# Ten convolution taps as products on ScalarE, added by VectorE, and a re-ordered head of the program

## The chip, the core and the metric

The kernel runs on one core of a Trainium2 chip. A core has TensorE (matrix products into PSUM, eight banks of 128x512 f32), VectorE, ScalarE, GpSimd, and SyncE, which issues most DMAs. Each engine runs its own instructions in order; they meet through semaphores. The metric is the device time of one execution, in microseconds (us); lower is better.

## The reference

Two transformer blocks on 256 tokens of width 1024, f32. Only what the change touches is shown: the first block's input projections, rotation and depthwise convolution of 31 taps over 512 channels.

```python
def conformer_conv(u, kernel, bias, ln_g, ln_b):
    a, b = jnp.split(u, 2, axis=-1)
    h = a * jax.nn.sigmoid(b)
    pad = CONV_WIDTH // 2
    h = lax.conv_general_dilated(h, kernel[:, None, :].astype(h.dtype), window_strides=(1,),
                                 padding=[(pad, pad)], dimension_numbers=('NWC', 'WIO', 'NWC'),
                                 feature_group_count=CONV_DIM) + bias
    hf = h.astype(jnp.float32)
    mu = jnp.mean(hf, axis=-1, keepdims=True)
    var = jnp.mean(jnp.square(hf - mu), axis=-1, keepdims=True)
    hn = (hf - mu) * lax.rsqrt(var + EPS) * ln_g + ln_b
    return jax.nn.silu(hn).astype(u.dtype)
...
        mod_x = (silu_c @ w_ada[i] + b_ada[i])[:, None, :]
        hx = modulate(rms_norm(x, norm1_g[i]), sh1, sc1)
        hc = modulate(rms_norm(ctx, norm1_g[i]), csh1, csc1)
        qx, kx, vx, ux = split_proj(hx @ w_in[i])
        kvc = hc @ w_in[i][:, ATT_DIM:3 * ATT_DIM]
        qx_rot = axial_rope(qx, row_pos, col_pos)
        kx_rot = axial_rope(kx, row_pos, col_pos)
        attn_x = neighbourhood_attention(qx_rot, qx, kx_rot, vx, kc, vc, rpb[i])
        conv_x = conformer_conv(ux, dw_kernel[i], dw_bias[i], conv_ln_g[i], conv_ln_b[i])
        x_new = x + g1 * (jnp.concatenate([attn_x, conv_x], axis=-1) @ w_out[i])
```

## The kernel before

Every large product is made in three: weights and activations are split into a high part (fp32r) and the rest, and TensorE adds high x high, high x low and low x high into one bank (`part`, lines 414 to 416). ScalarE makes the high part of each weight block (`hi`, line 1005), VectorE the low part (`lo`, line 1480). Weight blocks travel through a ring of six slots and their high buffers, in an order fixed by the list `slots`. A block is fetched by SyncE when the one before it in its slot has been used. TensorE's order is written out by hand, and so are those of VectorE and ScalarE.

The head goes by eight feature blocks of 128. For each, TensorE makes the modulation from an ada block of 1 MB (`mod_first`, line 454), VectorE copies the rows out (`rows_out`, line 1520), TensorE turns them (`mod_turn`, lines 465 and 468), VectorE applies them (`modulate_x`), ScalarE makes the high part (`high_x`), VectorE the low part (`low_x`), and TensorE uses the block for the convolution's two input halves a and b (`ab`, lines 490 to 496). Until the first weights are there, TensorE multiplies a tile of ones (`keep_busy`, line 476). After the eight blocks the context's rows are normalised (squares on ScalarE, line 1017; power on GpSimd; scaling `hat` on VectorE, line 1492) and the key weights are split.

Then TensorE runs the projections in this order: k of x, k of the context (KC), q, v of the context (VC), the first half of V. ScalarE copies each finished bank out, in the same order. Then TensorE turns KC, Q, KR and QR (line 396), two turns each, in banks 6, 7, 2, 3, 6, 7, 2, 3. A bank is free again when ScalarE has copied the turned tile: kcT (KC), qT (Q), kT (KR), qrT (QR). So KR's turn waits for kcT's copy, QR's for qT's. The first scores (`scores1(0)`, line 577) need all eight copies and stand between the two halves of the last product with V.

Beside all this the convolution runs on VectorE. `hp` holds the padded input by channel: 4 blocks of 128 channels, 288 columns. ScalarE makes tap 0 with the bias for each block (line 1074). VectorE adds the other 30 taps, each a fused multiply and add of 128x256 into `cacc`, four blocks in turn, 120 instructions (`taps`, line 1495). 20 follow the rotation of the keys (KR), 8 more the low parts of four weight halves, 52 the rotation of the queries (QR), 4 the first softmax step, and 36 are spread over the first five of eight attention steps.

Of the kernel before, what the change touches and what calls it, by code (L numbers as in the profile page):

```python
# [24 lines left out]
class Mem:  # L25


    def __init__(self, nc, ctx):
# [165 lines left out]
def weight_units(d, S):  # L194
# [70 lines left out]
    slots = [2, 4, 3, 5, 12, 0, 13, 1, 2, 4, 3, 5, 12, 0, 13, 1, 2, 3, 4, 5, 0, 1]  # L265
# [44 lines left out]
def pool_program(e, m, S, d):  # L310
    w = Waits(e)

    def power(i):
# [52 lines left out]
def tensor_program(e, m, S, by):  # L366
# [58 lines left out]
    def mod_unit(unit, k0, bk, sem):  # L425
# [19 lines left out]
    def mod_first(e8):  # L445
# [544 lines left out]
def scalar_program(e, m, S, units, by, out, d):  # L990
# [472 lines left out]
def vector_program(e, m, S, units, by):  # L1463
# [809 lines left out]
```

## Time and profile before

| | us |
|---|---|
| three timed runs | 736.58, 737.40, 737.42 (median 737.4) |
| profiled execution | 736.31 |
| its span on the core | 734.5 |
| TensorE busy | 722.9 |
| VectorE busy | 508.9 |
| ScalarE busy | 398.0 |
| GpSimd busy | 25.0 |
| granted TensorE clock, mean | 0.998 |

The profiled execution's own time lies 1.8 us above its span. A share of busy time tells how full an engine is, not whether it holds up the others. TensorE is full; only where it waits can an edit change the time, or where a new wait arises.

### The profile page before, as it was taken

What the parts mean: (1) busy time and instruction counts of PE and PEld (TensorE: products, weight loads), DVE (VectorE), ACT (ScalarE), POOL (GpSimd) and SP (SyncE); (2) the same over time, 40 slices, a digit from 0 to 9 for tenths busy, and PEclk for the clock granted to TensorE, in tenths of its full rate; (3) what the DMA queues carried; (4) which work ended last, traced back from release to release, by engine and by line L of the source; (5) the groups of instructions that cost most, each with busy time, mean ns of one, the idle gap of its engine ahead of it and who ended that gap; (6) DMA issues with size and microseconds to landing.
All of it is one profiled execution on the core that took longest, in us unless ns stands there. A gap on an engine that the chain in (4) does not pass through costs nothing.

```text
span 734.5 us, 9784 instructions
## 1 busy us (share of the span) xinstructions
PE 722.9 (98%) x3824; PEld 578.6 (79%) x3824; DVE 508.9 (69%) x924; ACT 398.0 (54%) x662; POOL 25.0 (3%) x44
## 2 busy tenths in 40 slices
PE   8989999999999999999999999999999999999996
PEld 7668885568888888888878777778888888888885
DVE  4678999889667555565988799865857445544544
ACT  3366337886666545556545677666466344334432
POOL 1030012000100000000010000000000000000000
PEclk9999999999999999999999999999999999999999
DMA  9993939945464655445538533344366555655511
GB/s 365 415 354 117 374 112 360 368 161 176 159 223 158 229 192 209 172 163 182 159 101 302 200 115 115 117 176 167 114 230 205 195 175 188 209 175 172 172 58 57
DMA packets 73741, 144.90 MB, mean 197 GB/s; under 512 B 4112, under 2 KB 27664, under 8 KB 72672
## 3 DMA queue, kind: packets, MB, share of 16 engines
q1 hardware_dynamic: 71888, 138.98, 54.6%
q0 software_dynamic: 1520, 5.03, 1.9%
q8 instruction: 30, 0.49, 0.3%
q10 hardware_dynamic: 288, 0.27, 0.1%
q14 instruction: 15, 0.12, 0.1%
HBM read 143.22 MB, written 1.05 MB: 196 GB/s over the span
## 4 chain that ended last, share of the span: by engine, by line
PE 93%; DVE 3%; issue 2%; ACT 1%; POOL 1%; POOLq 0%; DVEq 0%
PE bank L414 22%; PE bank L416 22%; PE bank L415 22%; PE bank L735 5%; PE bank L396 5%; PE bank L733 3%; PE bank L433 2%; PE bank L476 1%; PE bank L454 1%; PE bank L577 1%; PE bank L490 1%; DVE WL L1480 1%; PE bank L599 1%; PE bank L852 1%; PE bank L874 1%
## 5 line engine op out<-in xcount | busy, mean ns | idle before, releaser
L1480 DVE TENSOR_TENSOR WL<-W,WH 128x1024 fp32r<-128x1024 f32 (+2 forms) x222 | 249.5, 1169 | 48.8 <-ACT WH L1005 48.5
L1005 ACT ACTIVATE WH<-W 128x1024 fp32r<-128x1024 f32 (+2 forms) x222 | 211.7, 1011 | 52.9 <-DMA W<-in_w_mlp 40.5
L414 PE MATMUL bank<-WH,AHL 128*128 128x512 f32 (+1 forms) x480 | 189.2, 394 | 2.3 <-DVE WL L1480 2.0
L416 PE MATMUL bank<-WH,AHL 128*128 128x512 f32 (+1 forms) x480 | 185.4, 386 | 0.0
L415 PE MATMUL bank<-WL,AHL 128*128 128x512 f32 (+1 forms) x480 | 185.2, 386 | 0.0
L414 PEld LDWEIGHTS bank<-WH,AHL 128*128 128x128 f32 x480 | 90.2, 188 | 24.0 <-DVE WL L1480 3.5
L416 PEld LDWEIGHTS bank<-WH,AHL 128*128 128x128 f32 x480 | 90.1, 188 | 18.7
L415 PEld LDWEIGHTS bank<-WL,AHL 128*128 128x128 f32 x480 | 90.3, 188 | 16.8
L414 PE MATMUL bank<-WH,HH 128*128 128x512 f32 (+1 forms) x218 | 84.9, 390 | 0.0
L416 PE MATMUL bank<-WH,HL 128*128 128x512 f32 (+1 forms) x218 | 84.5, 388 | 0.0
L415 PE MATMUL bank<-WL,HH 128*128 128x512 f32 (+1 forms) x218 | 84.4, 387 | 0.0
L735 PE MATMUL bank<-AHL,WH 128*128 128x512 f32 x168 | 60.5, 398 | 0.0
L733 PE MATMUL bank<-AHL,WL 128*128 128x256 f32 x192 | 50.0, 281 | 0.0
L1495 DVE SCALAR_TENSOR_TENSOR cacc<-hp,vec,cacc 128x256 f32<-128x256 f32 x120 | 48.3, 475 | 0.0
L416 PEld LDWEIGHTS bank<-WH,HL 128*128 128x128 f32 x218 | 40.9, 188 | 8.5
L415 PEld LDWEIGHTS bank<-WL,HH 128*128 128x128 f32 x218 | 41.0, 188 | 8.3
L414 PEld LDWEIGHTS bank<-WH,HH 128*128 128x128 f32 x218 | 40.9, 188 | 8.0
L1412 ACT ACTIVATE rel<-bank 128x256 f32<-128x256 f32 x22 | 8.5, 384 | 62.2 <-PE bank L416 61.0
L1489 DVE TENSOR_TENSOR hid<-bank,rel 128x256 f32<-128x256 f32 x22 | 9.3, 424 | 42.2 <-ACT rel L1412 42.2
L733 PEld LDWEIGHTS bank<-AHL,WL 128*128 128x128 f32 x192 | 36.3, 189 | 2.0
L735 PEld LDWEIGHTS bank<-AHL,WH 128*128 128x128 f32 x168 | 31.6, 188 | 6.7
L1780 DVE TENSOR_TENSOR HL<-bank,HH 128x256 fp32r<-128x256 f32 (+1 forms) x26 | 11.1, 461 | 30.9 <-ACT HH L1013 30.9
(265 smaller groups left out, 831.4 us busy)
## 6 DMA issues: line engine op xcount, KB each, us to landing
W<-in_w_mlp SPq DMA_DIRECT2D x32, 1024.0 KB, 5.5
W<-in_w_in SPq DMA_DIRECT2D x24, 1024.0 KB, 5.1
W<-in_w_ada SPq DMA_DIRECT2D x12, 1024.0 KB, 8.0
WX<-in_w_ada SPq DMA_DIRECT2D x12, 1024.0 KB, 9.9
W<-in_w_gate SPq DMA_DIRECT2D x22, 512.0 KB, 4.2
W<-in_w_up SPq DMA_DIRECT2D x22, 512.0 KB, 5.3
W<-in_w_down SPq DMA_DIRECT2D x11, 1024.0 KB, 5.0
W<-in_w_out SPq DMA_DIRECT2D x8, 1024.0 KB, 5.1
```

Of the source, the lines that this page charges most:

```text
L396: ins = e.transpose(bank[b][:, c * 128:c * 128 + 128], src, m.ident[:, :])
L414: e.matmul(po, hs, wh[:, k, c0:c0 + cw], start=first and k == 0, stop=False)
L415: e.matmul(po, hs, wl[:, k, c0:c0 + cw], start=False, stop=False)
L416: ins = e.matmul(po, ls, wh[:, k, c0:c0 + cw], start=False, stop=last and k == unit.nk - 1)
L433: ins = e.matmul(bank[bk][32 * g:32 * g + 32, :], m.csp[:, k0 + g, :], wv[:, g, :], start=k0 == 0, stop=k0 == 4, tile_position=(0, 32 * g))
L733: ins = e.matmul(bank[4 + j][:, 0:256], wl[:, k, js], m.AH[:, 4 * i + k, :], start=False, stop=False)
L735: ins = e.matmul(both, wh[:, k, js], m.AHL[:, :, 4 * i + k, :], start=False, stop=i == 1 and k == 3)
L1005: e.activation(m.WH[unit.slot][:, c], m.W32[unit.slot][:, c], ACT.Copy).then_inc(S["w_hi"], 1)
L1480: e.tensor_tensor(m.WL[unit.slot][:, c], m.W32[unit.slot][:, c], m.WH[unit.slot][:, c].bitcast(F32), ALU.subtract).then_inc(S["w_lo"], 1)
L1489: e.tensor_tensor(o, a, b, op).then_inc(S[sem], 1)
L1495: e.scalar_tensor_tensor(o, a, scalar, b, op0, op1).then_inc(S[sem], 1)
L1780: e.tensor_tensor(L[:, k0:k0 + nj, ts], bank[b][:, 0:nj * 128].rearrange("p (j n) -> p j n", j=nj), H[:, k0:k0 + nj, ts].bitcast(F32), ALU ...
```

## The change

The convolution: taps 21 to 30 no longer run as 40 fused instructions. ScalarE makes each as four products of 128x256 (`tap_products`) into one of two buffers, `cprod`, and VectorE adds all four channel blocks with one addition of 128x1024 (`add_product`). Product n waits until addition n-2 has read the buffer. The buffers lie on memory that `U` and `V` use, so the copy of V waits for all ten additions. The products stand between ScalarE's bank copies. VectorE has 60 taps and the ten additions ahead of the first softmax, and 20 taps behind.

The head: the context is fetched two blocks earlier. ScalarE squares it ahead of feature block 6 and splits the key weights right behind block 7; VectorE scales its two halves ahead of block 7's row copy and between the low parts of the two key blocks. Five of the first 16 products of ones go, and the four behind the first ada block. Two slots change places in the list. Some semaphores are merged under new names, their counts moved accordingly (`gate_u` and `g_sig` to `gate_sig`, `kr` and `qr` to `rotated`, `eps` and `csp` to `setup`, `ones` and `hp_zero` to `fills`, `last_sum` and `x_g` to `last_rows`); those lines are left out here.

```diff
+        self.cprod = [M(f"cprod{i}", (68, 56)[i], [128, 4, 256]) for i in range(2)]
...
+CONV_PRODUCTS = 10
...
-    slots = [2, 4, 3, 5, 12, 0, 13, 1, 2, 4, 3, 5, 12, 0, 13, 1, 2, 3, 4, 5, 0, 1]
+    slots = [2, 4, 12, 5, 3, 0, 13, 1, 2, 4, 12, 5, 3, 0, 13, 1, 2, 3, 4, 5, 0, 1]
...
-    for n in range(16):
+    for n in range(14):
         load(n)
     e.dma_start(m.XC[:, :, :], d["ctx"].rearrange("(t p) n -> p t n", p=128)).then_inc(S["l_xc"], 16)
-    for n in range(16, len(units)):
+    for n in range(14, len(units)):
         load(n)
...
-    keep_busy(16)
+    keep_busy(11)
     mod_first(0)
-    keep_busy(4)
     mod_turn(0)
     keep_busy(8)
...
-    for k in range(8):
+    for k in range(6):
         hi()
         high_x(k)
     w.wait_ge(S["l_xc"], 16)
     for tb in range(2):
         square(2 + tb, m.XC[:, tb, :], m.XC2[:, tb, :])
     hi()
-    w.wait_ge(S["eps"], 1)
+    high_x(6)
     e.activation(m.stat[:, 92:93], m.stat[:, 94:95], ACT.Sigmoid)
+    hi()
+    high_x(7)
+    hi(2)
     for tb in range(2):
         w.wait_ge(S["b_mm"], 15 + tb)
-        e.activation(m.G[:, tb, :], bank[2 + tb][:, :], ACT.Sigmoid).then_inc(S["gate_u"], 1)
-    hi()
+        e.activation(m.G[:, tb, :], bank[2 + tb][:, :], ACT.Sigmoid).then_inc(S["gate_sig"], 1)
...
+    def tap_products(*ns):
+
+        for n in ns:
+            j = 31 - CONV_PRODUCTS + n
+            if n > 1:
+                w.wait_ge(S["conv_add"], n - 1)
+            else:
+                w.wait_ge(S["u_turned" if n == 0 else "c_turned"], (2, 4)[n])
+            for c in range(4):
+                e.activation(m.cprod[n % 2][:, c, :], m.hp[:, c, j:j + 256], ACT.Copy,
+                             scale=m.dw[:, c, j:j + 1]).then_inc(S["conv_prod"], 1)
+
+    tap_products(0, 1)
     for tb in range(2):
         from_bank("k_mm", 6 + 2 * tb, m.KC[:, tb, :], tb, slice(0, 512), "kc_out")
+        if tb == 0:
+            tap_products(2)
     hi(2)
+    tap_products(3)
     for tb in range(2):
         from_bank("q_mm", 2 + 2 * tb, m.Q[:, tb, :], 2 + tb, slice(0, 512), "q_out", 0.125)
+        tap_products(4 + 2 * tb, 5 + 2 * tb)
...
     for tb in range(2):
         from_bank("v_mm", 2 * tb + 2, m.VC[:, tb, :], 4 + tb, slice(0, 512), "vc_out")
+        tap_products(8 + tb)
     qk_features(0, m.kcT)
     qk_features(1, m.qT)
+    w.wait_ge(S["conv_add"], CONV_PRODUCTS)
     from_bank("v_mm", 6, m.V[:, 0, :], 0, slice(0, 512), "v_out")
     qk_features(2, m.kT)
     qk_features(3, m.qrT)
...
         low_x(k)
+        if k == 6:
+            mean_square(2, (2,))
+            hat(m.XC, m.XC2, 0, 2, "c_hat")
+    lo()
+    mean_square(3, (3,))
+    hat(m.XC, m.XC2, 1, 3, "c_hat")
+    lo()
     for tb in range(2):
-        mean_square(2 + tb, (2 + tb,))
-        hat(m.XC, m.XC2, tb, 2 + tb, "c_hat")
-    lo(2)
-    for tb in range(2):
-        w.wait_ge(S["gate_u"], tb + 1)
+        w.wait_ge(S["gate_sig"], tb + 1)
...
+    def add_product():
+
+        w.wait_ge(S["conv_prod"], 4 * conv["added"] + 4)
+        w.wait_ge(S["conv_first"], 4)
+        w.wait_ge(S["conv"], conv["n"] - 4)
+        w.wait_ge(S["conv_add"], conv["added"])
+        cv = flat(m.cacc[:, :, :])
+        tt(cv, cv, flat(m.cprod[conv["added"] % 2][:, :, :]), ALU.add, "conv_add")
+        conv["added"] += 1
...
-    rope1(m.KR, m.Kt, "kr")
-    taps(20)
+    rope1(m.KR, m.Kt, "rotated")
+    taps(8)
+    add_product()
+    add_product()
+    taps(8)
     lo(2)
+    add_product()
+    taps(4)
+    add_product()
+    w.wait_ge(S["q_out"], 2)
+    w.wait_ge(S["rotated"], 1)
+    rope1(m.QR, m.Q, "rotated")
+    for _ in range(4):
+        taps(6)
+        add_product()
     taps(8)
-    w.wait_ge(S["q_out"], 2)
-    w.wait_ge(S["kr"], 1)
-    rope1(m.QR, m.Q, "qr")
-    taps(52)
+    add_product()
+    add_product()
+    taps(8)
...
-        taps((9, 8, 8, 7, 4, 0, 0, 0)[u])
+        taps((6, 5, 4, 3, 0, 0, 0, 0)[u])
```

On ScalarE, from the first tap to the copy of the turned queries, this stood before (WH<-W are high parts of value weights):

```order
L1074 ACTIVATE cacc<-hp,vec 128x256 x4
L1013 ACTIVATE KC<-bank 128x512 x2
L1005 ACTIVATE WH_61<-W_0_49 128x1024 x2
L1005 ACTIVATE WH_62<-W_1_50 128x1024 x2
L1013 ACTIVATE Q<-bank 128x512 x2
L1013 ACTIVATE VC<-bank 128x512 x2
L1013 ACTIVATE kcT<-bank 128x512 x2
L1013 ACTIVATE qT<-bank 128x512 x2
L1013 ACTIVATE V<-bank 128x512
L1013 ACTIVATE kT<-bank 128x512 x2
L1013 ACTIVATE qrT<-bank 128x512 x2
```

In the changed kernel, from the second query copy on (products 4 and 5 stand ahead of it; `cprod_119` and `cprod_120` are the two product buffers):

```order
L1014 ACTIVATE Q<-bank 128x512
L1088 ACTIVATE cprod_119<-hp,vec 128x256 x4
L1088 ACTIVATE cprod_120<-hp,vec 128x256 x4
L1014 ACTIVATE VC<-bank 128x512
L1088 ACTIVATE cprod_119<-hp,vec 128x256 x4
L1014 ACTIVATE VC<-bank 128x512
L1088 ACTIVATE cprod_120<-hp,vec 128x256 x4
L1014 ACTIVATE kcT<-bank 128x512 x2
L1014 ACTIVATE qT<-bank 128x512 x2
L1014 ACTIVATE V<-bank 128x512
L1014 ACTIVATE kT<-bank 128x512 x2
L1014 ACTIVATE qrT<-bank 128x512 x2
```

Product 5 has moved in ahead of the second copy of Q, products 8 and 9 around the second copy of VC and so ahead of kcT.

On VectorE, from the end of the keys' rotation to the first softmax, before:

```order
L1489 TENSOR_TENSOR KR<-KR,tmp 128x1024
L1495 SCALAR_TENSOR_TENSOR cacc<-hp,vec,cacc 128x256 x20
L1480 TENSOR_TENSOR WL_55<-W_0_49,WH_61 128x1024 x2
L1480 TENSOR_TENSOR WL_56<-W_1_50,WH_62 128x1024 x2
L1495 SCALAR_TENSOR_TENSOR cacc<-hp,vec,cacc 128x256 x8
L1489 TENSOR_TENSOR QR<-Q,rope_78 128x1024
L1489 TENSOR_TENSOR tmp<-Q,rope_78 128x16x16 x4
L1489 TENSOR_TENSOR QR<-QR,tmp 128x1024
L1495 SCALAR_TENSOR_TENSOR cacc<-hp,vec,cacc 128x256 x52
```

In the changed kernel, from the end of the queries' rotation to the first softmax:

```order
L1517 SCALAR_TENSOR_TENSOR cacc<-hp,vec,cacc 128x256 x6
L1511 TENSOR_TENSOR cacc<-cacc,cprod_119 128x1024
L1517 SCALAR_TENSOR_TENSOR cacc<-hp,vec,cacc 128x256 x6
L1511 TENSOR_TENSOR cacc<-cacc,cprod_120 128x1024
L1517 SCALAR_TENSOR_TENSOR cacc<-hp,vec,cacc 128x256 x6
L1511 TENSOR_TENSOR cacc<-cacc,cprod_119 128x1024
L1517 SCALAR_TENSOR_TENSOR cacc<-hp,vec,cacc 128x256 x6
L1511 TENSOR_TENSOR cacc<-cacc,cprod_120 128x1024
L1517 SCALAR_TENSOR_TENSOR cacc<-hp,vec,cacc 128x256 x8
L1511 TENSOR_TENSOR cacc<-cacc,cprod_119 128x1024
L1511 TENSOR_TENSOR cacc<-cacc,cprod_120 128x1024
L1517 SCALAR_TENSOR_TENSOR cacc<-hp,vec,cacc 128x256 x8
```

Behind the rotation of Q there are now 40 taps and six additions where 52 taps were.

On VectorE at the end of the head, from the low part of feature block 7 on, before (XC is the context, `S_95` the features):

```order
L1489 TENSOR_TENSOR AHL<-S_95,AHL 128x256
L1506 TENSOR_SCALAR stat<-stat 128x1
L1492 TENSOR_SCALAR XC_109<-XC,stat 128x1024
L1506 TENSOR_SCALAR stat<-stat 128x1
L1492 TENSOR_SCALAR XC_109<-XC,stat 128x1024
L1480 TENSOR_TENSOR WL_57<-W_2_51,WH_63 128x1024 x2
```

In the changed kernel, with the first context scaling ahead of block 7's row copy:

```order
L1511 TENSOR_TENSOR AHL<-S_95,AHL 128x256
L1528 TENSOR_SCALAR stat<-stat 128x1
L1514 TENSOR_SCALAR XC_109<-XC,stat 128x1024
L1542 COPY rows_7_107<-bank 128x256
...
L1511 TENSOR_TENSOR AHL<-S_95,AHL 128x256
L1502 TENSOR_TENSOR WL_57<-W_2_51,WH_63 128x1024 x2
L1528 TENSOR_SCALAR stat<-stat 128x1
L1514 TENSOR_SCALAR XC_109<-XC,stat 128x1024
L1502 TENSOR_TENSOR WL_58<-W_3_52,WH_64 128x1024 x2
```

The scaling of the context has moved to either side: one ahead of `rows_7`, one between the low parts of the two key weight blocks.

## Rows read from the trace of the kernel before

**Rows 1.** The page, part 1: busy us (share of the span) xinstructions.
```profile
PE 722.9 (98%) x3824; PEld 578.6 (79%) x3824; DVE 508.9 (69%) x924; ACT 398.0 (54%) x662; POOL 25.0 (3%) x44
```

**Rows 2.** TensorE's waits: waiting line, releaser: us in total, times, longest.
```profile
PE bank L414 <- DVE WL L1480: 2.0, 1, 2.0
PE bank L490 <- ACT AHL L1013: 0.3, 1, 0.3
```

**Rows 3.** Busy us by engine (instructions), then clock, DMA share, GB/s; one stage.
```profile
57.45:101.99 44.54, 44.54 (x204) 36.91 (x203) 41.86 (x83) 18.11 (x28) 0.00 (x0) 1.00 0.60 216
```

**Rows 4.** Timeline of TensorE at the start: start us, us, engine, line, count.
```profile
2.76 6.40 PE L476 MATMUL bank<-ones 128*128 128x128 f32 x32 [2.76 <-POOL ones L334]
11.53 1.95 PE L476 MATMUL bank<-ones 128*128 128x128 f32 x16
```

**Rows 5.** Issue of the last ada block, and its us to landing.
```profile
27.14 0.43 SPq L294 DMA_DIRECT2D WX<-in_w_ada  x1
...
WX<-in_w_ada SPq DMA_DIRECT2D x1, 1024.0 KB, 9.4
```

**Rows 6.** Timeline, 41 to 50 us, of VectorE, ScalarE, TensorE; idle before in brackets.
```profile
41.23 0.42 DVE L1520 COPY rows<-bank 128x256 f32<-128x256 f32 x1
...
42.62 0.38 PE L468 MATMUL bank<-ident,rows 128*128 128x128 f32 x2
...
44.55 1.04 ACT L1017 ACTIVATE XC<-XC 128x1024 f32<-128x1024 f32 x1
...
46.53 0.75 DVE L1492 TENSOR_SCALAR XC<-XC,stat 128x1024 f32<-128x1024 f32 x1 [0.67 <-POOL stat L317]
...
48.68 2.35 DVE L1480 TENSOR_TENSOR WL<-W,WH 128x1024 fp32r<-128x1024 f32 x2
...
49.95 0.50 PE L414 MATMUL bank<-WH,AHL 128*128 128x512 f32 x1 [2.04 <-DVE WL L1480]
```

**Rows 7.** Timeline of VectorE in the convolution stage.
```profile
66.42 1.23 DVE L1489 TENSOR_TENSOR KR<-Kt,rope 128x1024 f32<-128x1024 f32 x1 [0.19 <-ACT Kt L1013]
...
69.02 1.22 DVE L1489 TENSOR_TENSOR KR<-KR,tmp 128x1024 f32<-128x1024 f32 x1
...
78.10 4.62 DVE L1480 TENSOR_TENSOR WL<-W,WH 128x1024 fp32r<-128x1024 f32 x4
...
86.49 1.22 DVE L1489 TENSOR_TENSOR QR<-Q,rope 128x1024 f32<-128x1024 f32 x1 [0.60 <-ACT Q L1013]
...
90.23 20.69 DVE L1495 SCALAR_TENSOR_TENSOR cacc<-hp,vec,cacc 128x256 f32<-128x256 f32 x52
```

**Rows 8.** Timeline of ScalarE in the same stage.
```profile
66.16 2.08 ACT L1074 ACTIVATE cacc<-hp,vec 128x256 f32<-128x256 f32 x4
...
85.86 0.60 ACT L1013 ACTIVATE Q<-bank 128x512 f32<-128x512 f32 x1 [4.84 <-PE bank L416]
...
102.62 1.09 ACT L1013 ACTIVATE kcT<-bank 128x512 f32<-128x512 f32 x2 [5.28 <-PE bank L396]
```

**Rows 9.** ScalarE's groups by form: names, shapes, count | busy us, mean ns.
```profile
L1005 ACT ACTIVATE WH<-W 128x1024 fp32r<-128x1024 f32 x202 | 200.8, 1052 | 48.9 <-DMA W<-in_w_mlp 40.5 <-DMA W<-in_w_up 3.8 <-DMA W<-in_w_in 2.7
...
L1005 ACT ACTIVATE WH<-W 128x512 fp32r<-128x512 f32 x16 | 9.1, 617 | 4.0 <-DMA W<-in_w_in 4.0
...
L1013 ACT ACTIVATE s<-s,rl 128x512 f32<-128x512 f32 x8 | 5.8, 724 | 3.4 <-DVE rl L1668 3.2
```

**Rows 10.** Timeline of TensorE around the turn of KR.
```profile
103.73 1.04 PE L396 MATMUL bank<-ident,KR 128*128 128x128 f32 x8
104.60 1.04 PE L396 MATMUL bank<-ident,QR 128*128 128x128 f32 x8
...
108.31 0.49 PE L577 MATMUL bank<-kT,qrT 64*128 64x256 f32 x2
```

**Rows 11.** Stages behind TensorE's last matmul, same columns as rows 3.
```profile
728.60:731.70 3.10, 0.00 (x0) 0.00 (x0) 1.88 (x6) 1.62 (x5) 0.55 (x1) 1.00 0.00 0
731.80:734.50 2.70, 0.00 (x0) 0.00 (x0) 0.00 (x0) 0.00 (x0) 0.00 (x0) 0.50 0.52 194
```

More of the change, by code:

```diff
@@ L138 @@
 NAMES = """l_cs l_x0 l_x1 l_vec l_id l_xc l_first l_b0 l_b1 l_b2 l_b3 l_second l_fg l_nf l_w0 l_w1 l_w2 l_w3 l_w4 l_w5 l_h2 l_h3 l_h4 l_h5
-l_out w_hi w_lo eps ones silu_c csp hp_zero
+l_out w_hi w_lo setup fills silu_c
 sq_sum mean_sq rstd ada1_mm rows1_dve rows1_turned mod1_sum mod1
 x_hat mx_dve mx_act kx c_hat c_turned mc_dve mc_act kc
-a_mm b_mm gate_u u u_turned hp conv_first conv k_mm q_mm v_mm k_out kc_out q_out v_out vc_out rope_mul kr qr qk_turned qk_act
+a_mm b_mm gate_sig u u_turned hp conv_first conv k_mm q_mm v_mm k_out kc_out q_out v_out vc_out rope_mul rotated qk_turned qk_act
 comb_r ada2_mm rows2 rows2_lo rows2_turned mod2_sum mod2
 bias_zero scores1 max1 exp1 rl1 p1_norm p1_norm_act p1_turned pt1 pv1
-conv_pair conv_block conv_sums conv_dve conv_act conv_rs k_conv a2
+conv_prod conv_add conv_pair conv_block conv_sums conv_dve conv_act conv_rs k_conv a2
 out_mm o1_hi o1_lo res1 nscale_dve nscale_act n_turned n_dve n_act kn
@@ L150 @@
 dot_mm dot_relu idx
-scores2 max2 exp2 rl2 p2_norm pr2_turned pt2 pv2 g_out g_sig
+scores2 max2 exp2 rl2 p2_norm pr2_turned pt2 pv2 g_out
 y_hi y_lo up_mm merge mrg_turned mrg_hi mrg_lo
-out2_mm res2 gu_mm dn_mm silu_g hid2 res3 last_sum x_g y_out y_act""".split()
+out2_mm res2 gu_mm dn_mm silu_g hid2 res3 last_rows y_out y_act""".split()
 LAST = (((0, 512), (512, 512)), ((0, 512), (512, 256), (768, 256)))
@@ L313, in power @@
     def power(i):
-        w.wait_ge(S["eps"], 2)
+        w.wait_ge(S["setup"], 2)
         w.wait_ge(S["mean_sq"], i + 1)
@@ L333, in pool_program @@
     e.dma_start(m.ident[:, :], d["ident"]).then_inc(S["l_id"], 16)
-    e.memset(m.ones[:, :], 1.0).then_inc(S["ones"], 1)
+    e.memset(m.ones[:, :], 1.0).then_inc(S["fills"], 1)
     power(0)
@@ L348, in pool_program @@
         e.dma_start(t, d[src]).then_inc(S["l_second"], 16)
-    w.wait_ge(S["eps"], 2)
+    w.wait_ge(S["setup"], 2)
     w.wait_ge(S["conv_dve"], 5)
@@ L429, in mod_unit @@
             take(bk)
-        w.wait_ge(S["csp"], 2)
+        w.wait_ge(S["setup"], 4)
         w.wait_ge(unit.landed[0], unit.landed[1])
@@ L449, in mod_first @@
         take(bk)
-        w.wait_ge(S["csp"], 2)
+        w.wait_ge(S["setup"], 4)
         w.wait_ge(by["ada1"][e8].landed[0], by["ada1"][e8].landed[1])
@@ L472, in keep_busy @@
     def keep_busy(count):
-        w.wait_ge(S["ones"], 1)
+        w.wait_ge(S["fills"], 1)
         for _ in range(count):
@@ L512, in tensor_program @@
         frees(tb, ("u", tb + 1))
-        frees(2 + tb, ("gate_u", tb + 1))
+        frees(2 + tb, ("gate_sig", tb + 1))
     def c_turn(i):
@@ L562, in tensor_program @@
     qk_turn(m.Q, 1, "q_out")
-    qk_turn(m.KR, 2, "kr", 1)
-    qk_turn(m.QR, 3, "qr", 1)
+    qk_turn(m.KR, 2, "rotated", 1)
+    qk_turn(m.QR, 3, "rotated", 2)
     def scores1(u):
@@ L627, in conv_mean @@
     def conv_mean():
-        w.wait_ge(S["ones"], 1)
+        w.wait_ge(S["fills"], 1)
         w.wait_ge(S["conv_block"], 1)
@@ L1070, in scalar_program @@
     w.wait_ge(S["hp"], 2)
-    w.wait_ge(S["hp_zero"], 2)
+    w.wait_ge(S["fills"], 3)
     w.wait_ge(S["u"], 2)
@@ L1124, in rows_copy @@
         w.wait_ge(S["ada2_mm"], 2 * u + 2)
-        w.wait_ge(S["qr"], 1)
+        w.wait_ge(S["rotated"], 2)
         if u:
@@ L1558, in low_quarter @@
         tt(two(L, i), two(hT, i), two(H, i).bitcast(F32), ALU.subtract, f"k{name}")
-    e.memset(col(94), -0.5).then_inc(S["eps"], 1)
-    e.memset(col(95), EPS).then_inc(S["eps"], 1)
-    e.memset(m.csp[:, :, :], 0.0).then_inc(S["csp"], 1)
+    e.memset(col(94), -0.5).then_inc(S["setup"], 1)
+    e.memset(col(95), EPS).then_inc(S["setup"], 1)
+    e.memset(m.csp[:, :, :], 0.0).then_inc(S["setup"], 1)
     w.wait_ge(S["silu_c"], 1)
-    w.wait_ge(S["csp"], 1)
-    e.tensor_copy(m.csp[:, :, 0:2], m.cs[:, :].rearrange("p (k r) -> p k r", r=2)).then_inc(S["csp"], 1)
+    w.wait_ge(S["setup"], 3)
+    e.tensor_copy(m.csp[:, :, 0:2], m.cs[:, :].rearrange("p (k r) -> p k r", r=2)).then_inc(S["setup"], 1)
     for tb in range(2):
@@ L1587, in vector_program @@
     lo(2)
-    conv = {"n": 4}
+    conv = {"n": 4, "added": 0, "last": [0, 0, 0, 0]}
     def taps(count):
@@ L1709, in conv_block @@
         else:
-            w.wait_ge(S["conv"], 120)
+            w.wait_ge(S["conv"], 120 - 4 * CONV_PRODUCTS)
+            w.wait_ge(S["conv_add"], CONV_PRODUCTS)
             w.wait_ge(S["v_mm"], 8)
@@ L2058, in merge_a @@
         hn = slice(512 * n, 512 * n + 512)
-        w.wait_ge(S["g_sig"], 1)
+        w.wait_ge(S["gate_sig"], 3)
         w.wait_ge(S["up_mm"], 2 * n + tb + 1)
@@ L2173, in vector_program @@
     w.wait_ge(S["sq_sum"], 24)
[L2174 removed]
+    e.tensor_scalar(col(39), col(22), col(23), EPS, ALU.add, ALU.add).then_inc(S["last_rows"], 1)
     w.wait_ge(S["res3"], 6)
[L2176 to L2177 removed]
+    tt(m.S1[:, 1, 768:1024], m.X[:, 1, 768:1024], m.g2b[:, 768:1024], ALU.mult, "last_rows")
+    w.wait_ge(S["last_rows"], 2)
     w.wait_ge(S["sq_sum"], 25)
```

23 lines of the change are left out of this document (10 added, 13 removed).

## The prediction, made before the changed kernel ran

> **What bounds the kernel now.** I read the busy times first. TensorE is busy for 722.9 of 734.5 us and VectorE for 508.9 [rows 1]. A matmul's end is modelled, so I then asked what TensorE waits for. There is almost nothing: 2.0 us once for a low part of the weights, 0.3 us once for a high part of the activations [rows 2]. The other 11.6 us are mostly ahead of its first matmul and behind its last. So two questions decide this change: which of these waits go, and whether a new one appears. Work taken from VectorE is worth nothing by itself, since TensorE never waits for VectorE between 57 and 150 us, although VectorE is busy for 41.86 of the 44.54 us up to 101.99 [rows 3].
>
> Durations below are from the profiled execution: its span is 734.5 us and its own time 736.31 us. The three timed runs are 736.58 to 737.42, up to 1.1 us above it.
>
> **The head.** TensorE opens with 16 matmuls on ones (32 records, 6.40 us [rows 4]). Five of them go, at 0.2 us a record up to 2 us, and four later ones. If its weights have landed by then, the first block can start that much earlier. The steps for feature blocks 6 and 7 take it back. The context now travels in place of the last ada block, which was issued at 27.14 and took 9.4 us, so it lands at about 36.5 [rows 5]. ScalarE then does two squares at 1.04 us [rows 6], about 2.1 with their reads, and one weight half-pair before the high part of block 6: 36.5 + 2.1 + 1.1 = 39.7, ready at 40.1, close to where it stood. VectorE gets the first context scaling (idle 0.67 for GpSimd's power, then 0.75) ahead of the row copy of block 7, which ran at 41.23; it moves by 1.4 us to 42.6, ends at 43.05, and TensorE, which used those rows at 42.62, now does so at about 43.1 [rows 6]. So block 7 ends 0.5 us later than before: 49.95 - 2.04 = 47.91 becomes 48.4. In return ScalarE has the first key weights split right after block 7, and VectorE makes their low part ahead of the second scaling. The 2.04 us wait in front of 49.95 goes. The key product starts at about 48.5 instead of 49.95: **1.5 us gained**. Bounds: 0 if block 7 slips by 2 us (the late context landing), 2.3 if it does not slip at all.
>
> **The convolution, part by part.** Forty fused taps leave VectorE. 52 of them take 20.69 us [rows 7], 0.397 each, so 15.9 us go. Ten additions of 128x1024 come. The row closest to one is the last instruction of the rotation, the same operation, shape and type: 1.22 us [rows 7]. An addition must wait until the tap before it is finished, and the next tap for it, which costs the overlap twice, so I take 1.37 for one between taps and 2.6 for a pair, 13.3 in all. Over the whole stage VectorE saves only 2.6 us. But the order decides. Before, 80 taps (31.8 us) stood ahead of the first softmax. Now 60 taps (23.8) and all ten additions (13.3) stand there: 37.1, or **5.3 us more** ahead of it.
>
> ScalarE gets 40 products of 128x256 with a scale from a tensor. No such row exists. Upper bound: the first tap, with scale and bias, four in 2.08 us, 0.52 each [rows 8]. Lower: a copy without a pointer; 1052 ns for 1024 columns and 617 for 512 [rows 9] give about 400 for 256, less the overlap of about 0.1 that stands between neighbours, 0.3. The copy scaled by a tensor takes 724 for 512 [rows 9], hence 0.51 for 256 and 0.40 as a step. I take 0.40, 1.6 us for one product of four. ScalarE has the time (18.11 busy of 44.54 [rows 3]). That would hide all of it, if it were not for the buffers: there are two, so product n waits until addition n-2 is done, and ScalarE issues in order. Whatever copy stands behind a product waits for VectorE too. The order of ScalarE shows what that is: the second query copy stands behind product 5, and the transposed context keys kcT stand behind product 9.
>
> I walk VectorE's chain with everything 1.5 us early. The rotation of the keys began at 66.42 and ended at 70.2 [rows 7], now 68.7. Eight taps and two additions: 68.7 + 3.2 + 2.6 = 74.5. Eight taps, 77.7. Four low halves at 4.62 together [rows 7], 82.3. Addition, four taps, addition: 82.3 + 1.25 + 1.6 + 1.3 = 86.4. Only now may product 5 run: 1.6, then the query copy 0.6 (it ran at 85.86 [rows 8]), 88.7. VectorE idles there for 2.2 us, where it idled 0.60 [rows 7]. Rotation of the queries, 3.8: 92.5. Four times six taps and an addition, 4 x (2.4 + 1.37) = 15.1: addition 8 is done at 107.6. Product 9 waits for it and takes 1.6, to 109.2; the first kcT copy ends at **109.8**.
>
> TensorE needs that copy to have the bank free for turning KR. It did that at 103.73 [rows 10], 1.5 earlier is 102.2. The copy had run at 102.62 [rows 8], in time. Now TensorE stands for 109.8 - 102.2 = **7.6 us**.
>
> A second wait follows. The copy of V must wait for all ten additions, since it writes over the second product buffer. 107.6 + 8 taps 3.2 + two additions 2.6 = 113.4. V, kT and qrT are five copies at about 0.5: 116.0. The scores need qrT; they began at 108.31 [rows 10]. From this side they are 7.7 us late. On TensorE's own side the turns and half a value product lie between: with kcT at 109.8 and qT a microsecond behind, it gets there at about 114.6, so this wait covers 1.4 us of slowness.
>
> **The clock** adds to that. With no matmul running the granted clock stayed at 1.00 from 728.6 to 731.7 and was at 0.50, 1.2 GHz, from 731.8 on [rows 11]. The wait of 7.6 us is more than twice as long as that first stretch, so I expect TensorE to come back at 1.2 GHz. At the start of the kernel 32 records took 6.40 us and 16 later ones 1.95 [rows 4]: 2.5 us lost until the clock was up. If the same is lost here, 1.4 of it is covered and 1.1 is not: 7.7 + 1.1 = **8.8 us**. If the clock stays up it is 7.7. The Trainium skill, "TensorE: Matmul & The Clock Gate", section "What's actually happening", states that the clock drops to half once the engine has been idle and rises only after sustained work. By that rule the turns with waits between them would not count as such work; what that gives is a rival below. The rows of before, with no inner pause longer than 2 us, can't show it.
>
> **Behind the scores** all is late by the same amount and TensorE has no wait to give back but 0.2 us, so what VectorE is spared in the eight attention steps (16 taps in four steps instead of 36 in five) hides in TensorE's time. Renamed semaphores and merged counters cost nothing: the values waited for are the same events. Span: 734.5 + 8.8 - 0.1, and 736.31 + 8.7 = 745.0. The timed runs lie some 0.3 to 1.1 above the profiled one, so I say **745.5 us**.
>
> **Rivals.**
> Clock down for longer. The turns and the whole half of the value product (103.73 to 108.31 [rows 10]) run at 1.2 GHz: about 4.6 us lost instead of 2.5, 2 us more, 747.5. For it: the turns come in pieces. Against: one start of the kernel took less.
> The head gives nothing. Block 7 waits for its rows and the ada block behind the context lands late. The chain of VectorE starts 1.5 later: 747. For it: the scaling stands right in front of the row copy. Against: two microseconds of wait have their cause removed.
> Cheap additions. If one took the 0.75 us of a scaling of the same 128x1024 [rows 6], ten save 4.7 us, kcT would come at 106 and the scores be 3 to 4 late: 740.5. Against it stands the 1.22 of the same instruction.
> Faster than before. ScalarE is not held up: kcT's copies are free when TensorE wants the bank, and the head's 1.5 us and the 0.2 remain: 735.8. It decides at one point: addition 8 must be done by 102.2 - 2.2 = 100.0, and my sum has 107.6. For it: 15.9 us leave the busiest helper, and ScalarE idles for 26 of 44 us. Against: eight additions, 11 us in my sum, would have to cost 3.
>
> **How the numbers follow.** Forecast, one long wait for kcT and one for the scores: 0.66, from 743.5 (clock up, head 2.3, product 0.3) to 747. Longer half clock 0.12, no gain in the head 0.10, cheap additions 0.06, faster 0.06. The range goes from 740.5, which takes in the cheap additions, to 749, where long half clock and lost head meet in part. A change within 0.2% (1.5 us) is what timing can't tell from none. Every case but the last is far beyond it: slower 0.93, faster 0.06, same 0.01.
>
> **What would show it.** In TensorE's waits: one of 7 to 8 us before the turn of KR, released by ScalarE's kcT copy, and 0 to 1.4 before the scores, released by qrT. The wait of 2.0 for WL gone. VectorE idle for about 2 us before the rotation of Q. ScalarE's products each beginning right behind an addition from the third on. A granted clock of 0.50 from about 106 to 115. Matmuls at 0.23 us steps again from 117. Wrong would be: kcT copied before 103, a product block near 1.0 or over 2.2 us, an addition under 1 us, or any other wait of TensorE over 1 us.

## The result, and the profile after

The changed kernel takes 744.27 us (median of four runs, 743.67 to 745.6), the kernel before beside it 737.41 (four runs, 736.58 to 738.12). The ratio is 1.0101, with a 95% interval of 1.0089 to 1.0113: slower by 6.6 to 8.3 us. Forecast was 745.5. The profiled execution took 743.67, with a span of 741.8: 7.3 more than before.

First the page's busy times, against [rows 1]:

```profile
PE 722.4 (97%) x3806; PEld 578.2 (78%) x3806; DVE 506.7 (68%) x894; ACT 414.8 (56%) x702; POOL 24.9 (3%) x44
```

TensorE does the same work in a longer span. VectorE is spared only 2.2 us, ScalarE has 16.8 more. What TensorE waits for, against [rows 2] (waiting line, releaser: total, times, longest):

```profile
PE bank L398 <- ACT kcT L1014: 7.8, 1, 7.8
PE bank L456 <- DMA W<-in_w_ada: 1.1, 1, 1.1
```

The wait of 2.0 for WL is gone. In its place stands one of 7.8 us that ScalarE's copy of kcT ends. Next TensorE's timeline (start, duration, engine, line, operation; idle time before it in brackets), which answers to [rows 6] at the end of the head and to [rows 10] at the turns:

```profile
42.66 0.44 PE L470 MATMUL bank<-ident,rows 128*128 128x128 f32 x2 [0.77 <-DVE rows L1542]
...
47.83 0.39 PE L416 MATMUL bank<-WH,AHL 128*128 128x512 f32 x1
...
99.49 1.04 PE L398 MATMUL bank<-ident,KC 128*128 128x128 f32 x8
100.36 1.04 PE L398 MATMUL bank<-ident,Q 128*128 128x128 f32 x8
109.22 1.94 PE L398 MATMUL bank<-ident,KR 128*128 128x128 f32 x8 [7.82 <-ACT kcT L1014]
...
112.52 0.74 PE L416 MATMUL bank<-WH,AHL 128*128 128x512 f32 x1
113.09 0.39 PE L417 MATMUL bank<-WL,AHL 128*128 128x512 f32 x1
...
115.70 0.70 PE L578 MATMUL bank<-kT,qrT 64*128 64x256 f32 x4
```

The key product starts at 47.83 instead of 49.95, the scores at 115.70 instead of 108.31. From there on all is 7.4 us late, and it stays so to within 0.1 us until the end. What ScalarE did meanwhile, against [rows 8]:

```profile
72.28 1.71 ACT L1088 ACTIVATE cprod<-hp,vec 128x256 f32<-128x256 f32 x4 [2.85 <-DVE cacc L1511]
...
85.62 1.71 ACT L1088 ACTIVATE cprod<-hp,vec 128x256 f32<-128x256 f32 x4 [1.32 <-DVE cacc L1511]
87.23 0.57 ACT L1014 ACTIVATE Q<-bank 128x512 f32<-128x512 f32 x1
...
106.89 1.70 ACT L1088 ACTIVATE cprod<-hp,vec 128x256 f32<-128x256 f32 x4 [1.64 <-DVE cacc L1511]
108.50 1.06 ACT L1014 ACTIVATE kcT<-bank 128x512 f32<-128x512 f32 x2
...
114.29 1.10 ACT L1014 ACTIVATE qrT<-bank 128x512 f32<-128x512 f32 x2
```

Read the brackets: from the third product on, every block of four but one waits for an addition (`<-DVE cacc`). The exception is product 3 at 78.17, which finds its buffer free behind the split of four weight blocks. The copy of kcT at 108.50 starts where the product of 106.89 ends. That product in turn started when this addition of VectorE was over, against [rows 7] and, for the row copy of block 7, [rows 6]:

```profile
42.19 0.42 DVE L1542 COPY rows<-bank 128x256 f32<-128x256 f32 x1
...
67.67 3.25 DVE L1517 SCALAR_TENSOR_TENSOR cacc<-hp,vec,cacc 128x256 f32<-128x256 f32 x8
71.02 2.55 DVE L1511 TENSOR_TENSOR cacc<-cacc,cprod 128x1024 f32<-128x1024 f32 x2
73.61 3.26 DVE L1517 SCALAR_TENSOR_TENSOR cacc<-hp,vec,cacc 128x256 f32<-128x256 f32 x8
...
87.84 1.23 DVE L1511 TENSOR_TENSOR QR<-Q,rope 128x1024 f32<-128x1024 f32 x1 [2.26 <-ACT Q L1014]
...
91.58 2.46 DVE L1517 SCALAR_TENSOR_TENSOR cacc<-hp,vec,cacc 128x256 f32<-128x256 f32 x6
...
95.40 2.46 DVE L1517 SCALAR_TENSOR_TENSOR cacc<-hp,vec,cacc 128x256 f32<-128x256 f32 x6
...
105.63 1.23 DVE L1511 TENSOR_TENSOR cacc<-cacc,cprod 128x1024 f32<-128x1024 f32 x1
...
110.26 2.55 DVE L1511 TENSOR_TENSOR cacc<-cacc,cprod 128x1024 f32<-128x1024 f32 x2
```

Last, the granted clock, against [rows 11] (stretch, length, busy us of PE, PEld, DVE, ACT, POOL, then clock, DMA share, GB/s):

```profile
101.40:106.20 4.80, 0.00 (x1) 0.00 (x0) 4.56 (x9) 2.21 (x6) 0.00 (x0) 1.00 0.00 0
106.30:113.00 6.70, 3.78 (x17) 3.81 (x18) 6.42 (x12) 3.80 (x9) 0.06 (x1) 0.50 0.00 1
113.10:116.00 2.90, 2.90 (x14) 2.17 (x14) 2.90 (x8) 2.88 (x6) 2.19 (x4) 1.00 0.30 90
```

It was at full speed for the first 4.9 us without a matmul, at 0.50 (1.2 GHz) from 106.3 to 113.0, and full again from 113.1.

### The profile page after: what moved, and what is told of

It is laid out like the page before. It is cut to its first block, busy times and chain, and to the rows that moved or that the text cites. A ratio compares the mean times of both kernels' runs of the same rounds, so it can differ in the third digit from the quotient of the medians.

```text
span 741.8 us, 9770 instructions
## 1 busy us (share of the span) xinstructions
PE 722.4 (97%) x3806; PEld 578.2 (78%) x3806; DVE 506.7 (68%) x894; ACT 414.8 (56%) x702; POOL 24.9 (3%) x44
## 4 chain that ended last, share of the span: by engine, by line
PE 83%; DVE 8%; ACT 3%; DMA 2%; issue 2%; POOL 0%; SPq 0%; POOLq 0%; DVEq 0%
PE bank L416 20%; PE bank L418 20%; PE bank L417 20%; PE bank L736 5%; PE bank L398 5%; PE bank L734 3%; DVE cacc L1517 2%; PE bank L435 2%; DMA XC<-in_ctx 1%; DVE cacc L1511 1%; DVE WL L1502 1%; PE bank L578 1%; PE bank L600 1%; DMA W<-in_w_ada 1%; PE bank L853 1%
## 5 line engine op out<-in xcount | busy, mean ns | idle before, releaser
L1517 DVE SCALAR_TENSOR_TENSOR cacc<-hp,vec,cacc 128x256 f32<-128x256 f32 x80 | 32.9, 479 | 0.2
```

What stands on the lines that cost most here:

```text
L1517: e.scalar_tensor_tensor(o, a, scalar, b, op0, op1).then_inc(S[sem], 1)
```

## Experiments

Nine further kernels ran. Times are medians, each with its ratio to the kernel before that ran beside it.

### Which part does it

**e1_head_only.** The changed head, the convolution as before:

```diff
-CONV_PRODUCTS = 10
+CONV_PRODUCTS = 0
...
     rope1(m.KR, m.Kt, "rotated")
-    taps(8)
-    add_product()
-    add_product()
-    taps(8)
+    taps(20)
     lo(2)
-    add_product()
-    taps(4)
-    add_product()
+    taps(8)
```

and so on to `taps(52)` and 36 taps in the attention steps, with ScalarE's products gone.

> The changed head, with the convolution as before (30 fused taps on VectorE, no products). My theory: the time is lost only in the convolution's chain of products and additions, and the head gains. In the changed kernel the turn of KC starts at 99.49 instead of 101.99, 2.5 us early, and nothing behind it is slow for another reason; so 737.4 - 2.5 = 734.9, span about 732. VectorE then enters the first softmax about 2.5 us early too, since its chain starts with the head. Rival (the head's gain is given back further on, by a weight block or a softmax step that is not early): 736.5 to 737.5.

Measured: 734.29 (733.83 to 735.24), ratio 0.9970 (0.9959 to 0.9982). The head alone is a gain of 2.2 us. TensorE's key product, its turn of KR, which it reaches with no wait, and the scores:

```profile
48.11 0.39 PE L416 MATMUL bank<-WH,AHL 128*128 128x512 f32 x1
...
101.55 1.04 PE L398 MATMUL bank<-ident,KR 128*128 128x128 f32 x8
...
106.15 0.70 PE L578 MATMUL bank<-kT,qrT 64*128 64x256 f32 x4
```

**e2_conv_only.** The head of before, the convolution changed. The first lines of its edit are shown; ScalarE's and VectorE's order at the end of the head is as before too:

```diff
-    slots = [2, 4, 12, 5, 3, 0, 13, 1, 2, 4, 12, 5, 3, 0, 13, 1, 2, 3, 4, 5, 0, 1]
+    slots = [2, 4, 3, 5, 12, 0, 13, 1, 2, 4, 3, 5, 12, 0, 13, 1, 2, 3, 4, 5, 0, 1]
...
-    for n in range(14):
+    for n in range(16):
...
-    keep_busy(11)
+    keep_busy(16)
     mod_first(0)
+    keep_busy(4)
```

> The convolution changed, the head as before. My theory: the chain of VectorE starts when the keys' rotation does, at 66.4 instead of 63.9, so its end and the scores come 2.5 us later than in the changed kernel: 744.3 + 2.5 = 746.8, with the same wait of about 8 us for kcT. Rival (the end of the chain is set by something that does not move with the head, the value weights' landing for one): 744 to 745, with a shorter wait.

Measured: 746.97 (746.13 to 747.7), ratio 1.0138 (1.0122 to 1.0154). The convolution alone costs 10.2 us. The two parts together, -2.2 and +10.2, make 8.0, inside the 6.6 to 8.3 of the whole. Its waits:

```profile
PE bank L398 <- ACT kcT L1015: 7.8, 1, 7.8
PE bank L416 <- DVE WL L1500: 2.1, 1, 2.1
```

The wait for kcT is the same 7.8 with either head, since VectorE's chain moves with the head as TensorE does. The old wait for WL is back. The whole loss comes from the convolution, and the head can't cure it.

### Which mechanism: the engine's order, or VectorE's load

**e3_kct_first.** Products 8 and 9 behind the copies of kcT and qT:

```diff
     for tb in range(2):
         from_bank("v_mm", 2 * tb + 2, m.VC[:, tb, :], 4 + tb, slice(0, 512), "vc_out")
-        tap_products(8 + tb)
     qk_features(0, m.kcT)
     qk_features(1, m.qT)
+    tap_products(8, 9)
     w.wait_ge(S["conv_add"], CONV_PRODUCTS)
```

> The changed kernel with products 8 and 9 moved behind ScalarE's copies of kcT and qT. Theory A (there are two gates in a row, and the second, the copy of V behind the tenth addition, is as late as the first): the turn of KR comes at about 103 instead of 109.2, TensorE's wait moves to the scores (from about 107 to 115.4), and the time stays at 744.3, from 743.5 to 746 with the clock falling there instead. Theory B (the place of kcT's copy behind product 9 is the cause by itself): the wait of 7.8 us goes and 737 or less is left.

Measured: 746.15 (745.42 to 748.35), ratio 1.0132 (1.0111 to 1.0153). TensorE's waits:

```profile
PE bank L578 <- ACT qrT L1014: 8.1, 1, 8.1
PE bank L398 <- ACT kcT L1014: 1.1, 1, 1.1
```

The same two waits on TensorE's timeline:

```profile
102.74 1.06 PE L398 MATMUL bank<-ident,KR 128*128 128x128 f32 x8 [1.14 <-ACT kcT L1014]
...
115.66 1.22 PE L578 MATMUL bank<-kT,qrT 64*128 64x256 f32 x4 [8.13 <-ACT qrT L1014]
```

The wait for kcT shrinks from 7.8 to 1.1, and an 8.1 us wait for qrT takes its place: theory A, though the time lies just above its 743.5 to 746. So both gates are real, and each alone holds the scores at the same time: 115.66 here, 115.70 in the changed kernel. The copy of V must follow the tenth addition in either order. The span is 743.7, 1.9 longer than that of the changed kernel, though the scores start at the same time. A window behind the turns shows why (columns as above):

```profile
109.90:120.00 10.10, 4.34 (x14) 3.04 (x15) 8.40 (x19) 5.34 (x10) 0.00 (x0) 0.50 0.23 90
```

The idle time now comes behind the turns instead of ahead of them, so the half clock falls on the scores and the products behind them, where nothing waits again and nothing covers it.

**e4_adds_close.** The same products and additions; the last six additions stand two taps apart, and the taps so freed move behind them:

```diff
     rope1(m.QR, m.Q, "rotated")
-    for _ in range(4):
-        taps(6)
+    for _ in range(6):
+        taps(2)
         add_product()
     taps(8)
-    add_product()
-    add_product()
-    taps(8)
...
-        taps((6, 5, 4, 3, 0, 0, 0, 0)[u])
+        taps((9, 8, 8, 7, 4, 0, 0, 0)[u])
```

> The same ten products, ten additions and 80 taps as the changed kernel, but only two taps between additions 5 to 10 and then eight, and the other 20 taps moved into the attention steps, where the kernel before had as many (9, 8, 8, 7, 4). Theory A (the order counts, not the work): from the rotation of the queries, done at 91.6, six times two taps and an addition, 6 x 2.2 = 13.2, put the tenth addition at 104.9 instead of 112.8; kcT waits for product 9, about 102.3, TensorE for 1 to 2 us; the scores begin near 107.5 instead of 115.7; time 744.3 - 8 = 736 to 737, about that of the kernel before. Rival (the additional work on VectorE and ScalarE costs, wherever it stands): 743 to 745.

Measured: 735.62 (735.47 to 738.15, ten runs), ratio 0.9988 (0.9978 to 0.9998). Against e1 beside it, 1.3 us are lost, and they stand in one row of TensorE's timeline:

```profile
102.96 1.06 PE L398 MATMUL bank<-ident,KR 128*128 128x128 f32 x8 [1.49 <-ACT kcT L1014]
...
107.73 0.70 PE L578 MATMUL bank<-kT,qrT 64*128 64x256 f32 x4
```

The additions 8 and 10 on VectorE:

```profile
99.37 1.23 DVE L1511 TENSOR_TENSOR cacc<-cacc,cprod 128x1024 f32<-128x1024 f32 x1
...
103.86 1.23 DVE L1511 TENSOR_TENSOR cacc<-cacc,cprod 128x1024 f32<-128x1024 f32 x1
```

More than eight of the ten microseconds come back without a single instruction less. The load of the engines is not the cause, the place of the additions in VectorE's order is. One relation ties the two kernels together: TensorE starts KR's turn 2.36 us behind the end of addition 8, which leaves room for one product (1.6) and the first of the two kcT copies. The changed kernel gives it (105.63 + 1.23 = 106.86, then 109.22), and this one gives the same (99.37 + 1.23 = 100.60, then 102.96), though its addition 8 comes 6.3 us earlier. More than two buffers were not tried.

### What the half clock costs

**e5_busy.** The changed kernel, with TensorE multiplying ones into a free bank while it would wait for kcT:

```diff
     qk_turn(m.Q, 1, "q_out")
+    take(1)
+    keep_busy(30, 1)
```

> The changed kernel with 30 more products of ones on TensorE, in a free bank, between the turns of Q and of KR, where it waits 7.8 us (60 records at 0.112, 6.7 us). It leaves nothing out. Clock theory: the granted clock no longer falls inside the wait; the turns of KR and QR take half as long, and TensorE is at the scores before 115.4, where qrT is copied. So the profiled span gains only 0.3 us (741.5), but the runs in which the half clock lasts longer go: the timed runs, 743.67 to 745.6 for the changed kernel, close up near 743.5, clock 0.998 in all. Rival (the spread and the loss have another cause): the runs stay between 743.7 and 745.6, or the added products delay KR's turn.

Measured: 744.66 (743.93 to 744.9), ratio 1.0104 (1.0088 to 1.0119). TensorE's timeline, and the clock from KR's turn to the scores:

```profile
101.41 6.86 PE L478 MATMUL bank<-ones 128*128 128x128 f32 x60
109.42 1.06 PE L398 MATMUL bank<-ident,KR 128*128 128x128 f32 x8 [1.14 <-ACT kcT L1016]
...
115.64 0.70 PE L580 MATMUL bank<-kT,qrT 64*128 64x256 f32 x4 [1.44 <-ACT qrT L1016]
```

In the window the columns are as above:

```profile
109.40:115.60 6.20, 4.79 (x28) 3.84 (x28) 5.96 (x12) 3.88 (x8) 2.35 (x4) 1.00 0.26 80
```

The clock is at 1.00 throughout, and KR's turn takes 1.06 instead of 1.94. TensorE is done with them and the half value product early, and then stands 1.4 us for qrT, to the same 115.64. From KR's turn to the scores TensorE's own work is 6.22 - 1.44 = 4.78 us here and 6.48 in the changed kernel. The half clock costs 1.7 us of TensorE's time, and the second gate covers 1.4 of it; 0.3 is left (6.48 less 6.22). The median is not lower, and the forecast that the runs close up near 743.5 failed: they spread from 743.93 to 744.9, with mean clocks of 0.995 to 0.999. What spreads them was not found.

### Is there something to win

**e6_head_hat.** e1, with the first context scaling behind block 7's row copy and its mean square ahead of it:

```diff
+        if k == 7:
+            mean_square(2, (2,))
         rows_out(k)
+        if k == 7:
+            hat(m.XC, m.XC2, 0, 2, "c_hat")
         modulation(k)
...
-        if k == 6:
-            mean_square(2, (2,))
-            hat(m.XC, m.XC2, 0, 2, "c_hat")
```

> The kernel with the changed head and the convolution of before (734.3), and in it the first scaling of the context moved: the mean square stays ahead of block 7's row copy, the scaling goes behind it, where VectorE waits for TensorE's turn anyway. Theory: TensorE waited 0.8 us for those rows; the copy starts at about 40.9 instead of 42.2, and the wait goes: 734.3 - 0.7 = 733.6. Rival (the scaling now stands ahead of block 7's reduction and costs there what it saved): 734.3.

Measured: 733.21 (733.13 to 733.33), ratio 0.9948 (0.9935 to 0.9960), with e9 the fastest kernel of this study. The row copy runs inside the time in which VectorE waited for GpSimd's power, first on VectorE's timeline:

```profile
40.68 0.42 DVE L1536 COPY rows<-bank 128x256 f32<-128x256 f32 x1
41.43 0.75 DVE L1508 TENSOR_SCALAR XC<-XC,stat 128x1024 f32<-128x1024 f32 x1 [0.33 <-POOL stat L319]
```

and the key product on TensorE's:

```profile
47.12 0.39 PE L416 MATMUL bank<-WH,AHL 128*128 128x512 f32 x1
```

TensorE's wait for the rows, 0.68 in e1, has gone, and the key product starts 0.99 us earlier than in e1 (48.11). A tenth of that is not the edit's: TensorE's own turn ahead of those rows stands at 41.79 here and at 41.89 in e1.

**e7_head_late_start.** e1 with the products of ones of the kernel before:

```diff
-    keep_busy(11)
+    keep_busy(16)
     mod_first(0)
+    keep_busy(4)
```

> The kernel with the changed head and the convolution of before (734.3), but with the 16 and 4 products of ones at the start as they were. The start was 0.9 us earlier in the changed kernel (second ada block at 12.52 instead of 13.40). Theory A: this earliness reached the key product, since block 7 had less to wait for than I thought: 734.3 + 0.9 = 735.2. Theory B (my prediction: the steps around blocks 6 and 7 take the early start back, and only the order of the head's end gains): 734.3 to 734.6.

Measured: 734.73 (734.32 to 734.78), ratio 0.9967 (0.9954 to 0.9979). VectorE's copy of block 7's rows in its profile:

```profile
42.20 0.75 DVE L1509 TENSOR_SCALAR XC<-XC,stat 128x1024 f32<-128x1024 f32 x1 [0.66 <-POOL stat L319]
42.87 0.42 DVE L1537 COPY rows<-bank 128x256 f32<-128x256 f32 x1
```

and TensorE's key product:

```profile
48.50 0.39 PE L416 MATMUL bank<-WH,AHL 128*128 128x512 f32 x1
```

It starts at 48.50. In the profiles of the changed kernel, e1, e3, e4 and e5, which have the changed head as it is, it starts between 47.83 and 48.11. So the early start brings the key product forward by 0.4 to 0.7 us, between the two theories. The times do not show it: the medians differ by 0.44, but e1 ran beside other runs of the kernel before, and the two ratios, 0.9967 and 0.9970, are the same within their intervals. The prediction gave the early start nothing.

**e8_four_products.** Products 0 to 3 only. Unlike products 4 to 9, none of them stands between the first copy of Q and kcT:

```diff
-CONV_PRODUCTS = 10
+CONV_PRODUCTS = 4
...
-        tap_products(4 + 2 * tb, 5 + 2 * tb)
...
-        tap_products(8 + tb)
...
     rope1(m.QR, m.Q, "rotated")
-    for _ in range(4):
-        taps(6)
-        add_product()
-    taps(8)
-    add_product()
-    add_product()
-    taps(8)
+    taps(44)
```

> The changed head with four products and additions (those ahead of the queries' rotation), 44 taps behind it, and the other 40 in the attention steps. None stands ahead of ScalarE's second query copy or of kcT. Theory: products that no copy of TensorE's chain waits behind cost nothing and, since TensorE does not wait for VectorE, gain nothing: 734.3, as without products (733.9 to 734.8). Rival (VectorE's relief shows once the stall is gone): under 733.8. Rival (any product costs): 735.5 or more.

Measured: 733.91 (733.62 to 736.77, seven runs), ratio 0.9969 (0.9955 to 0.9984), the same as e1. No wait for kcT. Sixteen taps off VectorE bring nothing, as TensorE never waited for them. Three of the runs lie at 735.6 to 736.8, and the profiled one (735.76) is among them. The stage of its start at the lower clock, with the columns as above:

```profile
11.00:14.30 3.30, 3.13 (x16) 3.10 (x16) 2.42 (x8) 1.32 (x3) 0.00 (x0) 0.50 1.00 415
```

Its clock fell for 3.4 us shortly after a wait of 1.86 for the first ada block. Its key product starts at 49.74, 1.6 us behind e1's; some 0.4 of that was there before the fall, since the first ada block was used at 9.59 instead of 9.14. The slowest run, 736.77, has a mean clock of 0.998, so such a fall explains at most the other two.

**e9_hat_ones.** e6 with 15 instead of 11 products of ones, to close the pause ahead of the first ada block:

```diff
-    keep_busy(11)
+    keep_busy(15)
     mod_first(0)
```

> The best kernel so far (changed head with the moved scaling, convolution of before, 733.2) with 15 products of ones ahead of the first block instead of 11. In one profile of the kernel with four products the granted clock was at 0.50 from 10.93 to 14.34, behind a start with a pause of 1.9 us, and 3 of its 7 runs lay 1.7 to 3 us higher. Theory: four more products of ones close that pause, at most 0.2 us later at the first block, and no run has such a second slow piece: 733.2, all runs within 0.4. Rival (the pause is harmless in this kernel, and the products only delay): 733.3 to 733.6 with the same spread.

Measured: 733.34 (733.02 to 733.7), ratio 0.9942 (0.9929 to 0.9956): no difference from e6. The expected gain in spread did not show, since the five runs of e6 had none to lose. Whether more ones protect against e8's fall stays open.

## Why the prediction was right, and where it was off

**The wait for kcT** was forecast at 7.6 us and measured at 7.8, on the path forecast: additions, product 9 behind addition 8, kcT behind product 9. e3 shows that the product ahead of the copy makes it, e4 that the taps between the additions do. VectorE's idle time ahead of the query rotation was forecast at 2.2 and measured at 2.26.

**Costs.** A product of four took 1.61 us from its start to the next instruction's (106.89 to 108.50; forecast 1.6), a step of 0.40 each. The Trainium skill, "ScalarE: Activation LUTs", section "What ACT_TABLE_LOAD costs", gives a base, an addition per pointer operand and an overlap that make 0.40 a step for this shape; the trace agrees, which leaves out the 0.30 and the 0.52 of the prediction's bounds. A single addition between taps cost 3.82 - 6 x 0.397 = 1.44 (95.40 less 91.58 on VectorE, forecast 1.37), a pair between taps 5.94 - 8 x 0.397 = 2.8 (73.61 less 67.67; forecast 2.6). So the chain from the keys' rotation to addition 10 took 45.1 us instead of 44.7.

**The head, mis-sized.** Forecast 1.5, measured 2.1 at the key product and 2.5 at KC's turn. The wait of 2.0 did go. The context landed at 36.4, as forecast at 36.5, but by luck: it was issued 0.9 us earlier than I took (26.23) and took 0.8 longer (10.2). The step that failed is that blocks 6 and 7 "take it back", the early start: they took back only part of it. I let the row copy of block 7 slip by 1.4 us from its old time, 41.23. But VectorE's work ahead of it moves with TensorE's start. Its row copy of block 6 ran 0.92 us earlier than before (35.90 against 36.82). Then it waited for ScalarE's high part of block 6, which stands behind the two squares and so behind the context's landing:

```profile
36.42 1.06 ACT L1018 ACTIVATE XC<-XC 128x1024 f32<-128x1024 f32 x1 [1.53 <-DMA XC<-in_ctx]
...
39.17 1.30 DVE L1502 TENSOR_TENSOR WL<-W,WH 128x512 fp32r<-128x512 f32 x2 [0.31 <-ACT WH L1006]
```

With the overlap lost by that wait, 0.51 of the 0.92 was left. From there the row copy of block 7 slipped by 1.47, close to the forecast 1.4, but to 42.19 and not to 42.6. With the early start the key product goes by that landing. Five profiles have the changed head as it is and kept the clock up in it; the squares of the context start at 36.42, 36.50, 36.53, 36.58 and 36.71 (the changed kernel, e4, e5, e3, e1), and the key product follows 11.40 to 11.44 us behind in every one (47.83, 47.90, 47.97, 47.99, 48.11). In e7, without the early start, the squares start at 36.40 and the key product only at 48.50, by TensorE's own blocks; that is the forecast 48.5. A context fetched still earlier was not tried. Another 0.4 us lies between the key product and KC's turn (51.66 us in the changed kernel and e7, 51.69 in e1, 52.04 before). All of it arises by the matmul behind the context's second turn: 49.95 to 57.45 is 7.50 us before, 48.50 to 55.63 is 7.13 in e7. What shortens that stretch was not tried.

**The clock, mis-sized.** Forecast: 2.5 us lost, 1.4 covered, 1.1 not. The cover was right to the decimal (e5: 1.44). Lost were only 1.7, so 0.3 were left. The price of 2.5 had been taken from one execution's start, where 32 records took 6.40 us [rows 4]. That row is no fixed price: the same 32 records took 5.47 in e7 and 5.20 in e2, by the same sum 1.6 and 1.3 lost. At the turns 3.9 us of work ran slowly, the turns and one matmul (109.22 to 113.09).

**The sum.** The scores were forecast 8.8 late and were 7.4 late. The difference of 1.4 is 0.8 of clock and 0.6 of VectorE's chain, which started 1.0 earlier, by the head, and was 0.4 longer. It is what the profiled execution (743.67 against 745.0) lies lower.

**The rivals.** "Cheap additions" fell: an addition took 1.22 to 1.23, not 0.75. "The head gives nothing" fell with e1. "Faster" fell, though it named the right place to decide it: addition 8. Its point of 100.0 was 1.0 late: TensorE is ready for KR at 101.4 (109.22 less the wait of 7.82) and starts 2.36 behind the addition, which makes 99.0. e4 has it done at 100.60 and waits 1.5 us. "Clock down for longer" did not happen in the profiled execution of the changed kernel. It did in e2, where 10 us at 0.50 followed the same wait:

```profile
108.10:118.20 10.10, 5.97 (x22) 5.46 (x23) 9.72 (x19) 6.14 (x14) 2.25 (x4) 0.50 0.03 11
```

There it cost about 1.3 us that nothing covered: qrT is copied by 118.4 and the scores start at 119.75, 7.52 us behind KR's turn instead of e5's 6.22. One run of the changed kernel, 745.6, had a mean clock of 0.991 where the other three had 0.993 to 0.995, and may be such a case; it has no trace of its own.

## What to carry to other kernels

When work moves to an engine that has time, list what is queued behind each moved instruction and ask what the moved instruction waits for: with two buffers the engine becomes a follower of the one that empties them, and every copy behind it is as late as that one. Find the second gate before removing the first (e3: 7.8 gone, 8.1 come), and put what frees buffers ahead of work that nobody waits for (e4: ten microseconds down to 1.3). Taking work from an engine that holds nobody up is worth nothing (e8); the gain sat in the order of a handful of instructions in the head (e1: 2.2 us, and 3.5 with e6's move).

## What the runs showed that was not expected

The time for which the clock stays up without a matmul is not fixed: 4.9 us in the changed kernel, about 3.7 in e2, 2.3 in e3. Nor is the time until it is back, counted from the first matmul after the wait: 3.9 us, 6.1 and 4.4. The Trainium skill, "TensorE: Matmul & The Clock Gate", section "What's actually happening", says that the count behind the clock does not start anew with the kernel, and that the point of change therefore varies by half a microsecond either way. That it varies, the three traces show too, though behind a wait and not at the kernel's start; their 2.3 to 4.9 us and 3.9 to 6.1 us are further apart than the page's figure. In e8 a wait of 1.86 us at the start was followed by a fall, while e5 with 1.8 us in the same place and the changed kernel with 1.1 kept their clock. A price for a lost clock should be a range: of the total it took 0.3 us in the changed kernel, 1.3 in e2 and 1.9 in e3, by how long the half clock lasted and by what waited behind it.
